# Second block's modulation sums in the first attention branch, and the second branch begun in the first's tail

## The reference, cut to what matters

```python
# first block
mod = split((silu(c) @ ada_w + ada_b), 6)
h = modulate(rmsnorm(x, norm_mix_g), mod[0], mod[1])
# two linear-attention branches over h (8 heads "hgrn", 4 heads "gla"), both directions in time
hq, hf_fwd, hf_bwd, hi, hg, gq, gk, gv, gg, gr_fwd, gr_bwd, m_hg, m_gla = split(h @ w_in)
glf = log_sigmoid(gr @ gk_w + gk_b) / 16          # gla: gates through a rank of 16
o = bidir(...)                                    # chunked scan: scores, states, outputs
y = sigmoid(m_hg) * (norm(o_hg) @ w_br_hg) + sigmoid(m_gla) * (norm(o_gla) @ w_br_gla)
x = x + mod[2] * (y @ w_o)
x = x + mod[5] * peer(modulate(rmsnorm(x, norm_ffn_g), mod[3], mod[4]), ...)   # experts
# second block: mla, ffn, ssm scan, ffn, each modulated by silu(c_2) @ mod_mix_w / mod_ffn_w + b
```

## Time and profile before

| | |
|---|---|
| Time, median of 3 runs | 3774.55 us (3766.69 to 3782.77) |
| The profiled execution's own time | 3763.8 us |
| Its span in the profile | 3761.8 us |
| TensorE (PE) busy | 3571.2 us, 95% of the span |
| Its weight loads (PEld) | 3090.7 us, 82% |
| VectorE (DVE) | 2357.4 us, 63% |
| ScalarE (ACT) | 1524.6 us, 41% |
| GpSimd (POOL) | 1026.3 us, 27% |
| First attention branch | about 57 to 487.5 us of the span |
| Second attention branch | 488 to 813 us |
| Experts' V stage | about 1902 to 2522 us |
| One head's turn in the first branch | 51.24 us |

### The profile page before, as it was taken

The page is one execution under the profiler, slowest core; times in us unless marked ns, Lnnn a source line. Parts: engine busy times, 40 slices in busy tenths (PEclk is TensorE's granted clock), DMA queues, the critical chain, the costliest instruction groups (busy, mean ns, idle before and its releaser), DMA issues. The chain is left out here.

```text
span 3761.8 us, 46713 instructions
## 1 busy us (share of the span) xinstructions
PE 3571.2 (95%) x18068; PEld 3090.7 (82%) x18068; DVE 2357.4 (63%) x3934; ACT 1524.6 (41%) x2054; POOL 1026.3 (27%) x678
## 2 busy tenths in 40 slices
PE   7999979979999999999999999999999998699998
PEld 6888867768878889999999999987778887678886
DVE  6655534444559998777757777666565476856354
ACT  5555535445342224444533333335442224434222
POOL 1222122127136775555421111110020014411002
PEclk9999989989999999999999999999999999899999
DMA  5111021026326675776599999961123322132331
GB/s 187 53 52 50 21 64 44 31 98 221 135 88 222 229 236 199 266 255 249 205 339 306 310 312 315 295 212 58 51 94 97 96 98 54 34 101 85 99 97 62
DMA packets 245131, 566.25 MB, mean 151 GB/s; under 512 B 91648, under 2 KB 133904, under 8 KB 242736
## 3 DMA queue, kind: packets, MB, share of 16 engines
q1 hardware_dynamic: 203968, 396.31, 32.8%
q0 software_dynamic: 37440, 135.32, 10.1%
q10 hardware_dynamic: 3504, 31.65, 2.1%
HBM read 497.36 MB, written 60.82 MB: 148 GB/s over the span
## 5 line engine op out<-in xcount | busy, mean ns | idle before, releaser
L1341 PE MATMUL peer_banks<-peer_h_parts,peer_w_parts 128*128 128x448 f32 (+1 forms) x3456 | 732.6, 372 | 12.1 <-POOL peer_w_parts L1622 6.2
L1341 PEld LDWEIGHTS peer_banks<-peer_h_parts,peer_w_parts 128*128 128x128 f32 x3456 | 645.9, 189 | 78.6 <-POOL peer_w_parts L1622 14.5
L1341 PE MATMUL peer_banks<-peer_act_parts,peer_w_parts 128*128 128x448 f32 x3072 | 624.5, 366 | 1.3 <-DVE peer_act_parts L2061 1.3
L1341 PEld LDWEIGHTS peer_banks<-peer_act_parts,peer_w_parts 128*128 128x128 f32 x3072 | 576.8, 188 | 46.6 <-DVE peer_w_parts L2066 1.6
L1794 ACT ACTIVATE peer_w_parts<-slots 128x1024 fp32r<-128x1024 f32 x272 | 287.1, 1055 | 428.5 <-PE peer_banks L1341 414.6
L1341 PE MATMUL ffn_ps<-h_parts,ffn_w_parts 128*128 128x512 f32 x1920 | 441.5, 393 | 18.1 <-DVE h_parts L2679 10.9
L1622 POOL TENSOR_TENSOR peer_w_parts<-slots,peer_w_parts 128x1024 fp32r<-128x1024 f32 x142 | 351.9, 2478 | 335.2 <-ACT peer_w_parts L1794 334.5
L1341 PEld LDWEIGHTS ffn_ps<-h_parts,ffn_w_parts 128*128 128x128 f32 x1920 | 363.3, 189 | 95.0 <-DVE ffn_w_parts L2517 15.6
L1341 PE MATMUL ffn_ps<-ffn_hidden,ffn_w_parts 128*128 128x512 f32 x1920 | 438.1, 390 | 1.5 <-DVE ffn_hidden L2586 1.5
L1341 PEld LDWEIGHTS ffn_ps<-ffn_hidden,ffn_w_parts 128*128 128x128 f32 x1920 | 360.4, 188 | 77.6 <-issue 3.1
L2363 ACT ACTIVATE ffn_w_parts<-slots 128x1024 fp32r<-128x1024 f32 x160 | 168.5, 1056 | 311.1 <-PE ffn_ps L1341 303.7
(11 more groups left out here) (579 smaller groups left out, 5673.2 us busy)
## 6 DMA issues: line engine op xcount, KB each, us to landing
slots<-in_peer_u SPq DMA_DIRECT2D x128, 512.0 KB, 3.7
slots<-in_peer_v SPq DMA_DIRECT2D x128, 512.0 KB, 4.9
slots<-in_mlp_w SPq DMA_DIRECT2D x128, 512.0 KB, 3.5
peer_slab<-in_w_mod POOLq DMA_DIRECT2D x96, 512.0 KB, 5.5
peer_acts<-h SPq DMA_DIRECT2D x128, 224.0 KB, 4.1
peer_gates<-peer_slab ACTq DMA_DIRECT2D x16, 1792.0 KB, 15.4
peer_slab<-peer_acts SPq DMA_DIRECT2D x128, 224.0 KB, 5.1
peer_slab<-peer_gates SPq DMA_DIRECT2D x128, 224.0 KB, 5.5
```

The lines of the kernel that those rows point to most:

```text
L1341: last = nc.tensor.matmul(out, w(a, k), x(b, k), start=start and k == ks[0] and n == 0, stop=stop and k == ks[-1] and n == 2)
```

## The change

Three things.

1. The 96 sums leave the `V` stage of `peer`. The loads, the row, the silu, the sums and the bias now lie in the hgrn phase. SP issues the loads in its own queue behind the weight loads (from weight 8 on, three for each), into four slots, two of them the ring of the coming gla phase. VectorE makes the sums in turns 1 to 7 in bursts of 4, 4, 3 and 3. The silu is ScalarE's sigmoid in turn 0 and VectorE's product at the start of turn 1.
2. gla's memory and some of its semaphores are laid out ahead (`heads_memory`, object `early`, called `nxt` in the hgrn phase), and both phases share the projection banks (`K.heads_ps`). In hgrn's last turns the low-rank weights and first two weight tiles of gla are loaded and split, the 48 low-rank matmuls are laid beside the last head's small matmuls (one step of three after each step of `beside` from `f0` on), and the gates of gla's first head are made.
3. gla starts with these ready: SP and GpSimd begin with tile 2, TensorE with the first product.

The diff, cut to its core:

```diff
@@ heads_phase, SP
+            def load_mod(n):
+                if n == 1:
+                    sp.wait_ge(nxt.row_silu, 1)
+                if n == 2:
+                    sp.wait_ge(h_lo, 2 * KT)
+                if n >= 4:
+                    sp.wait_ge(nxt.mod_done, n - 3)
+                sp.dma_start(nxt.mod_slots[n % 4], d["w_mod"][48 + n]).then_inc(nxt.mod_in[n % 4], 16)
...
-            for m in range(R if hg else 0, heads * NW):
+            for m in range(R if hg else 2, heads * NW):
                 if m >= R:
                     sp.wait_ge(w_lo, m - R + 1)
                 sp.dma_start(ring[m % R], w_dram[m]).then_inc(ready[m % R], 16)
+                while nxt is not None and asked < min(MOD2, 4 + 3 * (m - 8)):
+                    load_mod(asked)
+                    asked += 1
+            if nxt is not None:
+                sp.wait_ge(nxt.zeroed, 1)
+                sp.dma_start(nxt.wgr[:]..., d["w_gr"]...).then_inc(nxt.gr_in, 16)
+                for dr in range(2):
+                    sp.dma_start(nxt.gw[16 * dr:16 * dr + 16, dr, :], d["gk_w"][dr]).then_inc(nxt.gr_in, 16)
+                sp.wait_ge(nxt.mod_done, MOD2)
+                for m in range(2):
+                    sp.dma_start(nxt.ring[:, m, :], d["w_gla"][m]).then_inc(nxt.ready[m], 16)
@@ GpSimd
+            if nxt is not None:
+                nc.gpsimd.memset(nxt.gw[:], 0.0).then_inc(nxt.zeroed, 1)
...
+                for m in range(2):
+                    g.wait_ge(nxt.w_hi, m + 1)
+                    nc.gpsimd.tensor_tensor(nxt.wp[:, m, 1, :], nxt.ring[:, m, :], nxt.wp[:, m, 0, :]..., ALU.subtract).then_inc(nxt.w_lo, 1)
@@ TensorE
-                if H == 0 and dr == 0:
-                    pe.wait_ge(gr_stored, 1)
+            def next_ranks():      # 16 steps of 3 matmuls, over hp and hcp; yields between
+            def next_gates():      # after gr_stored: 4 matmuls, gla's z0 and z1 of head 0
-                    if lora:
+                    if lora and H:
                         low_rank(H, 0)
                         low_rank(H, 1)
-                for _ in pace:
+                fill = next_ranks() if nxt is not None and it == heads else iter(())
+                begun = False
+                for r in pace:
+                    begun = begun or r == "f0"
+                    if begun:
+                        next(fill, None)
+                for _ in fill:
                     pass
+                if nxt is not None and it == heads + 1:
+                    next_gates()
@@ ScalarE, hgrn
+                    if h == heads - 1:     # before evict_keys(h, 0)
+                        act.wait_ge(nxt.gr_in, 48)
+                        A(nxt.wgp[:, 0, :], nxt.wgr[:], ACT.Copy).then_inc(nxt.gr_hi, 1)
+                    if h == heads - 1:
+                        next_high(0)       # after evict_keys(h, 0); next_high(1) after evict_keys(h, 1)
+                    if it == 0:
+                        act.wait_ge(nxt.row_in, 16)
+                        A(nxt.mod_slots[1], nxt.mod_row[:], ACT.Sigmoid).then_inc(nxt.row_sig, 1)
...
+                if hg and h == heads - 1:  # at the turn's end
+                    act.wait_ge(nxt.gr_done, 1)
+                    A(nxt.gr[:, T:N], pg[0:32, 2 * T:2 * T + TC], ACT.Copy)
+                    A(nxt.gr[:, 0:T], pg[0:32, 0:T], ACT.Copy).then_inc(nxt.gr_stored, 1)
@@ VectorE
+            def modulate(k):
+                for n in range(asked[0], min(MOD2, asked[0] + k)):
+                    slot = nxt.mod_slots[n % 4]
+                    dve.wait_ge(nxt.mod_in[n % 4], 16 * (n // 4 + 1))
+                    V.scalar_tensor_tensor(out=slot, in0=slot, scalar=1.0, in1=nxt.mod_row[:], op0=ALU.mult, op1=ALU.mult,
+                                           accum_out=K.mod[:, 48 + n:49 + n]).then_inc(nxt.mod_done, 1)
+                asked[0] = min(MOD2, asked[0] + k)
...
+                turn = hg and 0 < it < heads
+                if hg and it == 1:
+                    dve.wait_ge(nxt.row_sig, 1)
+                    V.tensor_tensor(nxt.mod_row[:], nxt.mod_row[:], nxt.mod_slots[1], ALU.mult).then_inc(nxt.row_silu, 1)
+                    dve.wait_ge(nxt.row_silu, 1)
+                if turn:
+                    modulate(4)            # burst A
                 if g is not None:
                     finish(g)
                 if h is not None:
                     query_decay(h)
                     mask(h, 0)
                 if hg:
+                    if turn:
+                        modulate(4)        # burst B
                     if H is not None:
                         forget(H, 0)
                     if h is not None:
                         gates(h)
                         states(h, 0)
+                    if turn:
+                        modulate(3)        # burst C
                     if H is not None:
                         forget(H, 1)
                         differences(H, 0)
                     if h is not None:
                         mask(h, 1)
+                    if turn:
+                        modulate(3)        # burst D
                     if H is not None:
                         differences(H, 1)
                         products(H, 0)
@@ peer, GpSimd
-            g.dma_start(M.rows[:, 0, :], d["c_rows"][2].partition_broadcast(P)).then_inc(M.rows_in, 16)
-            for s in range(MG):
-                g.dma_start(M.ring[:, s, :], d["w_mod"][48 + s]).then_inc(M.ready[s], 16)
...
-                    g.dma_start(M.ring[:, s, :], d["w_mod"][i * MG + s + 48 + MG]).then_inc(M.ready[s], 16)
-            M.finish(g, nc.gpsimd, M.multiplied)
+            for c in range(BEFORE, CALLS):
+                fetch_down(c)
@@ peer, VectorE
-                if n % 4 and m < M.tiles:
-                    M.dot(dve, m)
-                    m += 1
```

More of the change, by code:

```diff
@@ L396, with heads_memory, heads_phase @@
 NPR = T // PR
-def heads_phase(nc, K, d, name, w_dram, heads, vt, gate_norm, y, scan_scale, lora=False):
+MOD2 = 4 * 24
+def heads_memory(ph, hg, vt):
+    N = T + TC
+    m = Consts()
+    if not hg:
+        m.ring = ph.sb("ring", [P, 3, KT * P])
+    m.wp = ph.sb("w_parts", [P, 2, 2, KT * P], F32R)
+    m.lg = ph.sb("log_gate", [P, 2, N])
+    m.key = ph.sb("key", [P, 2 if hg else 1, N])
+    m.q_sb = ph.sb("q", [P, T])
+    m.v_sb = ph.sb("v", [P, vt, N])
+    m.g_sb = ph.sb("g", [P, vt, T])
+    m.sgate = ph.sb("sgate", [P, vt, T])
+    m.cum = ph.sb("cum", [P, 2, N])
+    m.e_q = ph.sb("e_q", [P, 2, T])
+    m.e_k = ph.sb("e_k", [P, 2, T])
+    m.e_kd = ph.sb("e_kd", [P, 2, N])
+    m.e_x = ph.sb("e_x", [P, 2, T])
+    m.q_dec = ph.sb("q_dec", [P, 2, T])
+    m.e_last = ph.sb("e_last", [P, 2, NPR])
+    m.vtok = ph.sb("vtok", [P, N // P, vt, P])
+    m.ktok = ph.sb("ktok", [P, 2, N // P, P])
+    m.score = ph.sb("score", [P, 2, T])
+    if not hg:
+        with ExitStack() as alias:
+            m.wgr = alias.enter_context(ph.nc.sbuf_tensor("gla_wgr", [P, KT * 32], F32))
+            m.wgp = alias.enter_context(ph.nc.sbuf_tensor("gla_wgr_parts", [P, 2, KT * 32], F32R))
+            mod_ring = alias.enter_context(ph.nc.sbuf_tensor("mod2_ring", [P, 2, D], F32))
+            m.mod_row = alias.enter_context(ph.nc.sbuf_tensor("mod2_row", [P, D], F32))
+            m.mod_slots = [mod_ring[:, 0, :], mod_ring[:, 1, :], m.ring[:, 0, :], m.ring[:, 1, :]]
+    m.state = ph.sb("state", [P, 2, NPR, vt * P])
+    m.osq = ph.sb("osq", [P, T])
+    m.rstd = ph.sb("rstd", [P, T])
+    if not hg:
+        m.na = ph.sb("na", [P, N])
+        m.gw = ph.sb("gw", [32, 2, T])
+        m.gr = ph.sb("gr", [32, N])
+        m.ready = ph.sems(*[f"w_ready{i}" for i in range(3)])
+        m.w_hi, m.w_lo, m.proj_done = ph.sems("w_hi", "w_lo", "proj_done")
+        m.mod_in = ph.sems(*[f"mod2_in{i}" for i in range(4)])
+        m.row_in, m.row_sig, m.row_silu, m.mod_done, m.mod_biased = ph.sems(
+            "mod2_row_in", "mod2_row_sig", "mod2_row_silu", "mod2_done", "mod2_biased")
+        m.gr_in, m.gr_hi, m.gr_lo, m.gr_done, m.gr_stored, m.zeroed = ph.sems(
+            "gr_in", "gr_hi", "gr_lo", "gr_done", "gr_stored", "zeroed")
+    return m
+def heads_phase(nc, K, d, name, w_dram, heads, vt, gate_norm, y, scan_scale, lora=False, early=None, nxt=None):
     hg = not lora
@@ L687, in low_rank @@
                 M(con(n), w, gr[:, T:N], start=True, stop=True).then_inc(proj_done, 1)
[L689 to L690 removed]
+            def next_ranks():
+                pe.wait_ge(nxt.gr_lo, 1)
+                pe.wait_ge(stored, heads * NT)
                 for out, src in ((pg[0:32, 0:T], hp), (pg[0:32, 2 * T:2 * T + TC], hcp)):
[L692 to L694 removed]
+                    for k in range(KT):
+                        last = parts_product(nc, out, lambda a, k: nxt.wgp[:, a, k * 32:(k + 1) * 32], lambda a, k: src[:, a, k, :],
+                                             (k,), k == 0, k == KT - 1)
+                        if k < KT - 1 or src is hp:
+                            yield
```

(16 more changed lines are left out.)

103 lines of the change are left out of this document (39 added, 64 removed).

## The result

The changed kernel takes 3803.95 us (median of 5 runs, 3800.48 to 3806.79), the kernel before beside it 3774.55 (3760.88 to 3783.95): a ratio of 1.008, 95% interval 1.0051 to 1.0109. It is slower: the interval leaves out 1. The profiled execution is 3806.79 (span 3805.1) against 3763.8 (span 3761.8): the span is 43.3 us longer. The medians differ by 29.4 only, because the profiled execution of before was a short one for its kernel and that of after a long one; more on the scatter stands at the end. Every ratio here is an estimate over the runs of both kernels and need not be the quotient of the two medians.

The account below looks back on a forecast made before the run. TensorE was taken as the bound nearly everywhere except the seam. Stalls +37.6, clock +9, seam -18 and loads 0 gave +28.6 on 3763.8, so 3792.4; with 10.75 up to the runs' median, 3803 us, range 3757 to 3835.

Parts of the forecast that it names:

- The removal beside the experts: Expert stage: taking out the 96 sums and loads gains 0, bounds -2 and 0 us, since TensorE never waits there.
- Bursts A and B: First branch: 4 sums each, at the turn's start and ahead of the forget gate, hidden in gaps of 9.5 and 5.3 us.
- C: First branch, after the first states: 3 sums, 0.6 us late for the second gate, whose second instruction meets GpSimd's subtraction.
- D: First branch, ahead of the second direction's differences: 3 sums where VectorE had no idle time, meeting a GpSimd subtraction.
- The walk of a full turn: First branch, turns 2 to 6: late VectorE states make TensorE stand 5.6 us a turn, bounds 1 to 8.
- rival 1: First branch: GpSimd does not hold the sums, so 1.8 us a turn; 3773 us, no change; chance 0.18.
- Turn 1: First branch, turn 1: the row's silu and loads that begin only then push the second burst late; 8 us.
- The clock: TensorE's clock after six stalls in the first branch: 1.5 us lost at each, +9 in all, bounds 0 and 15.
- Loads and queues: The 96 loads in SP's queue between the first branch's weight loads: 0, up to +20 us if landings are far slower.
- Rival 3: First branch: slow landings into four slots set the pace, stalls of about 11 us a turn; 3840 us; chance 0.12.
- The seam: Between the two branches: gap 26.0 to 2.3 us, tail 7.5 longer, first product 1.8 gained; net -18, bounds -12 and -24.
- Rival 4: Seam: tail grows 11 us and the product gains nothing, so 12.7 saved; 3808 us; shares the forecast's chance of 0.58.

Follow-up runs that it names:

- no-hold kernel: The changed kernel with GpSimd's subtraction in the first branch replaced by a short memset that reads nothing; 3751.45 us, ratio 0.9954.
- loads-only kernel: The changed kernel with each of the 96 sums run over 8 of 1024 columns, loads and waits kept; 3753.42 us, ratio 0.9962.
- seam alone: The changed kernel with the 96 sums and their loads back beside the experts, the second branch's early start kept; 3753.91 us, ratio 0.995.
- turn 1 spared: The changed kernel with bursts 4, 4, 2, 4, the last behind the second states; turn 1's first burst dropped, two sums ending turn 7; 3756.4 us.
- one sum ahead: The changed kernel with two of the last burst's three sums moved behind the second direction's states; 3773.03 us, ratio 1.0008.
- sums alone: The changed kernel with its sums in the first branch, but the second branch beginning as before, after the barrier; 3823.9 us, ratio 1.0145.
- bursts moved: The changed kernel with bursts of 4, 4, 2 and 4, the last behind the second direction's states; 3767.91 us, ratio 0.9986.

## Why the prediction was right, and where it was off

The mechanism came as forecast, and so did the median (3803 against 3803.95). Between the two profiled executions, the sum's own ground, +28.6 was forecast and +43.3 came, so the good median is partly luck: it was reached from 3774.55, a median of three runs of before, while 50 later runs of before have medians of 3768.34 and 3768.14. Against those the change is slower by 35.7. Step by step:
- **The removal beside the experts, 0.** Right: 3754.02 without any sums, 3753.91 with them there. The experts' second products take 625.4 us before (1901.8 to 2527.2) and 624.0 after (1945.6 to 2569.6): -1.4, inside the bounds of -2 and 0 (first matmul's start to last's).
- **Bursts A and B, hidden.** Right from turn 2 on: with both in place, C at two sums and D moved, no output stall is left there but the last head's.
- **The walk of a full turn, 5.6.** It is 5.81 to 5.83. It can be followed step by step in turn 3, 24.3 us later than in the earlier trace rows: D was to start at 233.9 and starts at 233.7 on that clock, the products at 243.7 and 243.5. The held second sum, forecast to take some 3.3 us, takes 3.41; the held products are in the trace too. The 3.41 alone rules out rival 1, and the no-hold kernel shows its price: 0.7 us a turn without any hold.
- **Turn 1, 8.** 7.57 at the output and 2.54 more at an earlier matmul of the same turn (136.93, waiting for the keys that ScalarE evicts): 10.1. The sum of the output stalls was forecast as 37.6; the waits row has 38.4.
- **The clock, +9.** This is the term that was mis-sized. From one turn's first output to the next it was 51.24 us; after, the six periods from 155.17 to 508.27 sum to 353.1. Less 6 x 51.24 and less the 30.8 of stalls in them, 14.8 is left, above my 9. Up to turn 1's outputs (141.85 before, 155.17 after) it is 13.3 us; less the two stalls of 10.1, 3.2 is left. Of it 1.4 stands before any sum is made (the third weight's products start at 81.25 instead of 79.88), and 1.7 is the clock after the stop of 2.54, 0.72 over 6 us. Busy time of TensorE in the 6 us behind that stop and behind the output stalls of turns 1 and 3, with the granted clock third from the end:
```profile
136.93:142.93 6.00, 6.00 (x26) 0.72 0.07 29
155.17:161.17 6.00, 6.00 (x25) 0.50 0.12 31
274.55:280.55 6.00, 6.00 (x37) 0.76 0.17 34
```
All 6 us at half clock lose 3.0; at 0.76 they lose 1.4. Turns 2, 4, 5 and 6 have 0.67, 0.53, 0.69 and 0.50. The six together lose 14.1, nearly the whole of the 14.8. My price, 1.5 a stall, came from one stop of before, whose 0.62 over 4 us is near the mildest of these six. With what follows it, a stall of 5.8 us among dense matmuls costs 7.3 to 8.8 us here.
- **Loads and queues, 0.** Right but for turn 1: the loads-only kernel has one stall of 1.5 us there and a product start 1.3 us later than without loads. Rival 3 is out.
- **The seam.** The gap fell from 26.0 to 1.7: 24.3 saved, 23.7 forecast. The tail from turn 7's outputs to the last output grew by 6.1 (7.5 forecast): from 38.1 (449.40 to 487.53) to 44.3 (508.27 to 552.54). The first product gained 0.2 us (7.33 to 7.10), not 1.8: TensorE stood 3.86 us before it, and the granted clock over the product is 0.79, where it was 0.77. In all the seam brings 24.3 less 6.1 and 0.2 more, 18.4, where 18 was forecast. Rival 4's 12.7 is out. With the seam alone the product starts 17.3 earlier.

Added up at the product start: 58.9 to turn 7's outputs, + 6.1 - 24.3 = +40.7 (30.4 by the forecast's terms). The remaining +2.6 to the end is about what the second branch took more (259.4 against 256.7 us from its first product to the last one's start). That lies within its scatter: 254.8 to 262.3 us over these ten kernels.

## What to carry to other kernels

Work put into a busy engine's program is priced by its place, not by the engine's busy share: with 3 sums of burst D ahead of the state that TensorE waits for, the same 96 sums start the second branch's products 58.0 us later than the seam alone (554.3 against 496.2; 50 us by the medians). With D behind that state, C shorter by one and turn 1 spared, they cost nothing that shows (495.9). Walk the queue instruction by instruction against the partner that can hold it. Each us of lateness may run into the next hold, so lateness comes in steps: 2.3 us of sums moved away brought 4.5. And look first at whether the place left behind was a bound: here it wasn't, so that only the seam had anything to give.

## What the runs showed of the hardware

**What a short stall costs beyond itself.** A stall of 1.3 us (one sum ahead) leaves the granted clock at 1.00 (window 200 to 300: 96.05 busy at 1.00), and so does one of 1.73 (turn 7 of the changed kernel). Stops of 2.5 us went both ways in turn 1: after 2.54 (changed kernel) and 2.46 (sums alone) the clock is 0.72 over the next 6 us, after 2.48 (one sum ahead) it is 1.00. The stalls of 5.1 to 7.6 us looked at are each followed by the half clock for some 3 us up to the whole of the next 6, which adds a quarter to a half to a stall of 5.8. Which of the two it is varied from turn to turn of one program at the same stall of 5.8; what decides it isn't settled here.

**What a hold takes in.** Beside a subtraction of GpSimd a scan of VectorE is held (3.99), as the differences, the products and the two-input sums are. The no-hold kernel shows that it depends on what GpSimd does: no sum was held beside a memset (longest 1226 ns), though a memset (236.00, 0.96 us) began in the middle of one sum and the next sum (236.58, 1.22 us) in the middle of that memset. A one-input tensor_scalar is another case: started with a memset (227.33) it took 1.36 us instead of 0.56, and a memset that began in the middle of one (271.22) took 1.27 us instead of 0.95. The Trainium skill (SBUF — State Buffer, section "SBUF: two separate sides") says that whoever starts second waits out the whole instruction, and that a VectorE instruction with two SBUF inputs takes the lock only against a GpSimd instruction that reads SBUF, one in a two-port mode against any. Both agree here: the subtraction reads SBUF, the memset reads nothing. That the tensor_scalar runs in a two-port mode is not shown by any run.

**Two lengths of the experts' second products.** This is one source of the runs' scatter. In ten profiled executions these 3072 matmuls keep TensorE busy for either 624 to 625 us or 636 to 637, at the same granted clock of 1.00 and with no more than 1.3 us idle, whatever the program. The source view of the turn-1-spared kernel, and of that without sums (lengths in ns, first and last start):
```profile
L1459 PE MATMUL peer_banks<-peer_act_parts,peer_w_parts x3072: 357/369/448, 1883.9 to 2520.2; 128*128 128x448 f32 x192
```
```profile
L1439 PE MATMUL peer_banks<-peer_act_parts,peer_w_parts x3072: 358/365/447, 1890.9 to 2515.1; 128*128 128x448 f32 x192
```
And one stretch of each, of TensorE alone (busy, clock, DMA share, GB/s): 486 against 496 matmuls in 100 us.
```profile
2200.00:2300.00 100.00, 100.00 (x486) 1.00 0.72 225
```
```profile
2200.00:2300.00 100.00, 100.00 (x496) 1.00 0.72 228
```
Neither has the sums or their loads beside the experts, and the DMA share is the same. The kernel before has both there and the short length, that with the seam alone has both there and the long one. So the sums and their loads don't decide it. The cause stays open. The times of most kernels fall into two groups 10 to 14 us apart (3753 to 3758 and 3767 to 3772 with the bursts moved), which would fit this, though only profiled executions show it. It can't be all: the profiled executions of the sums alone and of turn 1 spared have the long length, and yet each kernel has runs 6 to 10 us slower. The second branch scatters by 7.5 us as well. Before and after were both profiled at the short length, so in this the 43.3 compares like with like. Of the five runs of before beside the changed kernel, two (3782.77 and 3783.95) lie in its upper group (3779 to 3783 in the set of 32) and the median between the two; that is why 29.4 is less than 35.7.
